# Two output projections finished by token halves: norm sums, broadcasts and the first scaled tiles moved in among the products

## The reference

```python
# first block
h = h + concat([y_attn, y_ret]) @ w_out          # output projection, 1024 x 1024
m = rms_norm(h, ffn_norm_w)
h = h + (silu(m @ w_gate) * (m @ w_up)) @ w_down
# second block
...
h = h + memory_cross_attention(c, m, w_q_cross, w_kv_cross, w_o_cross)  # its last product: 512 x 1024
f = rmsnorm(h, g_ffn)
h = h + (silu(f @ w_gate) * (f @ w_up)) @ w_down
return rmsnorm(h, g_final)

def rms_norm(x, w):
    return x * rsqrt(mean(x * x, -1) + EPS) * w
```

## Time and profile before

| | |
|---|---|
| median of three runs | 2857.78 us |
| the profiled execution | 2857.05 us |
| its span in the trace | 2854.9 us |
| PE busy in the span | 2759.4 us, 97% |
| VectorE busy | 1580.7 us, 55% |
| GpSimd busy | 1333.7 us, 47% |
| ScalarE busy | 911.2 us, 32% |
| mean granted TensorE clock | 0.987 of full speed |

### The profile page before, as it was taken

One profiled execution on the slowest core, in us unless ns is written; L12 is line 12 of the kernel. 1 busy time (PEld: TensorE's weight loads), 2 busy tenths in 40 slices (PEclk: granted clock), 3 DMA queues, 4 the chain that ended last, 5 costly groups with the idle time before them and its releaser, 6 DMA issues. The chain is left out here.

```text
span 2854.9 us, 36940 instructions
## 1 busy us (share of the span) xinstructions
PE 2759.4 (97%) x13908; PEld 2231.2 (78%) x13908; DVE 1580.7 (55%) x2437; ACT 911.2 (32%) x1777; POOL 1333.7 (47%) x1012
## 2 busy tenths in 40 slices
PE   7999999999999999999999899999899999999997
PEld 6777788778888888787766688878787788888886
DVE  6776654865555555613367731243378655555556
ACT  5644431332222322324344410021243322223223
POOL 3322334466656666532222244546614665566653
PEclk9999999999999999999999999999999999999998
DMA  3010111112111111220111011132100111111111
GB/s 132 30 38 31 42 68 39 44 52 63 48 50 54 52 59 52 80 76 30 38 30 32 29 52 52 51 118 67 60 30 30 59 60 45 52 52 55 61 48 67
DMA packets 71376, 151.96 MB, mean 53 GB/s; under 512 B 6448, under 2 KB 29360, under 8 KB 70064
## 3 DMA queue, kind: packets, MB, share of 16 engines
q1 hardware_dynamic: 64256, 123.76, 13.6%
q10 hardware_dynamic: 6960, 26.01, 2.4%
HBM read 141.36 MB, written 8.39 MB: 52 GB/s over the span
## 5 line engine op out<-in xcount | busy, mean ns | idle before, releaser
L650 POOL TENSOR_TENSOR WH<-WRAW,CST 128x512 fp32r<-128x512 f32 x204 | 228.8, 1121 | 874.6 <-PE PS L775 750.1
L773 PE MATMUL PS<-XH,WH 128*128 128x512 f32 x1248 | 513.0, 411 | 2.8 <-DVE XL L2104 2.8
L775 PE MATMUL PS<-XH,WL 128*128 128x512 f32 x1248 | 489.7, 392 | 0.0
L774 PE MATMUL PS<-XL,WH 128*128 128x512 f32 x1248 | 489.0, 392 | 0.0
L684 POOL TENSOR_TENSOR WL<-WRAW,WH 128x512 fp32r<-128x512 f32 x216 | 309.9, 1435 | 272.7 <-ACT WH L1732 271.7
L2543 DVE TENSOR_TENSOR H<-H,PS 128x512 f32<-128x512 f32 x352 | 236.3, 685 | 161.7 <-PE PS L1097 159.3
L773 PEld LDWEIGHTS PS<-XH,WH 128*128 128x128 f32 x1248 | 235.3, 189 | 82.8 <-issue 36.3
L1095 PE MATMUL PS<-HH,WH 128*128 128x512 f32 x704 | 275.5, 391 | 5.3 <-DVE HL L2477 5.3
L1732 ACT ACTIVATE WH<-WRAW 128x512 fp32r<-128x512 f32 x204 | 129.4, 634 | 471.4 <-PE PS L1097 382.9
L652 POOL TENSOR_TENSOR WL<-WRAW,WH 128x512 fp32r<-128x512 f32 x204 | 271.6, 1331 | 16.0
L775 PEld LDWEIGHTS PS<-XH,WL 128*128 128x128 f32 x1248 | 235.4, 189 | 52.0
(11 more groups left out here) (334 smaller groups left out, 4989.4 us busy)
## 6 DMA issues: line engine op xcount, KB each, us to landing
WRAW<-ws SPq DMA_DIRECT2D x104, 512.0 KB, 3.5
WRAW<-ws SPq DMA_DIRECT2D x176, 256.0 KB, 2.6
RAWX<-ws SPq DMA_DIRECT2D x88, 256.0 KB, 2.7
H<-xT ACTq DMA_DIRECT2D x4, 1024.0 KB, 10.9
H<-xT ACTq DMA_DIRECT2D x2, 2048.0 KB, 11.0
h_spill<-H ACTq DMA_DIRECT2D x1, 4096.0 KB, 11.2
H<-h_spill ACTq DMA_DIRECT2D x4, 1024.0 KB, 8.0
outT<-H ACTq DMA_DIRECT2D x4, 1024.0 KB, 4.4
```

Source lines behind the costliest of these rows:

```text
L650: pool.tensor_tensor(WH[:, j, c], WRAW[:, j, c], ONES[:, 0:1].to_broadcast((P, 512)), ALU.mult).then_inc(hi_split, 1)
L773: pe.matmul(out, WH[:, j, w], rh(kt), start=(n == 0), stop=False)
L774: pe.matmul(out, WH[:, j, w], rl(kt), start=False, stop=False)
L775: last = pe.matmul(out, WL[:, j, w], rh(kt), start=False, stop=(n == len(kts) - 1))
```

## The change

Three things, in both transitions:

- The last two units go by halves of the tokens. In the first projection (6,0), (7,0), (6,1), (7,1); in the cross projection the units n = 2 and 3 run all their h = 0 tiles, then all their h = 1 tiles (`CROSS_OUT`, the order for all three engines).
- `norm_sums(k, 0)` and `norm_spread(k, 0)` go in among the products of h = 1 of these units, `norm_sums(k, 1)` from behind the last unit to kt 2 of `plain(0)`, and `norm_spread(k, 1)` from kt 3 to kt 6. Root and inverse of h = 1 go from piece 2 to piece 5.
- The scaled pieces 0 and 1 are taken out of the feed-forward loop (`plain_scale`, `plain_high`): piece 0's scale before the last tile's result is added, piece 1's scale and piece 0's low part between that addition and the last addition of squares. ScalarE makes high part 0 before the last square and high part 1 after it.

In the cross projection ScalarE's table for the square root is also loaded ahead of the tiles, and `add_squares` waits for its own last addition.

```diff
@@ pe
             def norm_sums(k, h):
-                pe.wait_ge(summed, 2 * h + 2 if not k else 16 * k + 4 if h else 16 * k - 4 if k in (2, 5) else 16 * k + 3)
+                pe.wait_ge(summed, 2 * h + 2 if not k else 16 * k + 4 if h else 16 * k + (0, 2, -4, 3, 0, -4)[k])
...
                 for h in range(2):
-                    unit_half(u0 + 6, h)
-                last_unit(u0 + 7, k)
+                    for u in (u0 + 6, u0 + 7):
+                        def hook(kt):
+                            if (u, h, kt) == (u0 + 6, 1, 4):
+                                norm_sums(k, 0)
+                            if (u, h, kt) == (u0 + 7, 1, 2):
+                                norm_spread(k, 0)
+
+                        unit_half(u, h, hook)
...
-                            if b == 0 and h == 0 and kt == 3:
+                            if (b, h, kt) == (0, 0, 2):
+                                norm_sums(k, 1)
+                            if (b, h, kt) == (0, 0, 6):
                                 norm_spread(k, 1)
...
+                def hook(kt):
+                    if (n, second, h, kt) == (2, 0, 1, 0):
+                        norm_sums(4, 0)
+                    if (n, second, h, kt) == (3, 1, 1, 2):
+                        norm_spread(4, 0)
...
-            norm_spread(4, 0)
-            norm_sums(4, 1)
+            for n, second, h in CROSS_OUT:
+                if (n, second, h) != (0, 0, 0):
+                    cross_out(n, second, h)
@@ act
-                for t in (6, 7):
-                    for h in range(2):
+                for h in range(2):
+                    for t in (6, 7):
                         bank = 2 * ((u + t) % 2) + h
                         square(t, h, bank, uses[u + t][bank])
                         if (t, h) == (7, 0):
                             norm_root(k, 0)
+                        if h:
+                            plain_high(t - 6)
...
-                for n in range(16):
-                    kt, h = n % 8, n // 8
-                    if n == 2:
+                for n in range(2, 16):
+                    if n == 5:
                         norm_root(k, 1)
...
+                    plain_high(n)
...
+            load_sqrt()
+            for n, second, h in CROSS_OUT:
@@ dve
+            def plain_scale(k, gain, n):
+                if n < 16:
+                    kt, h = n % 8, n // 8
+                    if n == 5:
+                        norm_inverse(k, 1)
+                    if kt == 0:
+                        dve.wait_ge(spread, 2 * k + h + 1)
+                    dve.scalar_tensor_tensor(out=scaled_input(kt, h), in0=H[:, kt, half(h)], scalar=v(gain + kt),
+                                             in1=PS[:, OB + h], op0=ALU.mult, op1=ALU.mult).then_inc(scaled, 1)
+                    nsc.n += 1
+                if n:
+                    kt, h = (n - 1) % 8, (n - 1) // 8
+                    if n == 16:
+                        dve.wait_ge(scaled, nsc.n)
+                    xh, xl = plain_input(kt, h)
+                    low(xl, scaled_input(kt, h), xh)
...
-                    for t in (6, 7):
-                        for h in range(2):
+                    for h in range(2):
+                        for t in (6, 7):
                             bank = 2 * ((u0 + t) % 2) + h
                             add_result(t, h, bank, uses[u0 + t][bank])
-                            add_squares()
+                            if (t, h) == (7, 1):
+                                plain_scale(k, gain, 1)
+                            add_squares(h)
                             if (t, h) == (7, 0):
                                 norm_inverse(k, 0)
+                            if (t, h) == (6, 1):
+                                plain_scale(k, gain, 0)
...
+                if (n, second, h) == (3, 0, 1):
+                    plain_scale(4, V_GFFN, 1)
+                add_squares(h)
+                if (n, second, h) == (2, 1, 1):
+                    norm_inverse(4, 0)
+                if (n, second, h) == (3, 1, 1):
+                    plain_scale(4, V_GFFN, 0)
```

More of the change, by code:

```diff
@@ L548, in program @@
         U2V, VV, C21, C22 = (XX[:, HALF * n:HALF * (n + 1)] for n in range(4))
+        CROSS_OUT = ([(n, second, h) for n in (0, 1) for second in (1, 0) for h in range(2)]
+                     + [(n, second, h) for h in range(2) for n in (2, 3) for second in (1, 0)])
         def raw(r):
@@ L2055, in _ @@
             split_cross(1)
-            for n in range(4):
+            load_sqrt()
+            for n, second, h in CROSS_OUT:
                 u = U_CO + n
[L2060 to L2065, removed]
+                bank = 4 + h if second else 2 * (u % 2) + h
+                square(2 * n + second, h, bank, uses[u][bank])
+                if (n, second, h) == (3, 0, 0):
+                    norm_root(4, 0)
+                if (n, h) == (3, 1):
+                    plain_high(1 - second)
             ffn(1, 4)
@@ L2087, in link, with add_squares @@
                 dve.wait_ge(dve_step, nst.at())
-            def add_squares():
-                h = nsm.n % 2
+            def add_squares(h=None):
+                sq = nsm.n % 2
+                h = sq if h is None else h
                 dve.wait_ge(squared, nsm.at() + 1)
-                dve.tensor_tensor(ACC[:, h], ACC[:, h], SQ[:, h], ALU.add).then_inc(summed, 1)
+                dve.wait_ge(summed, nsm.at())
+                dve.tensor_tensor(ACC[:, h], ACC[:, h], SQ[:, sq], ALU.add).then_inc(summed, 1)
                 nsm.n += 1
@@ L2417, in residual @@
                     nsm.end(3)
[L2418 to L2419 removed]
+                    for h in range(2):
+                        for t in (6, 7):
                             bank = 2 * ((u0 + t) % 2) + h
                             add_result(t, h, bank, uses[u0 + t][bank])
[L2422 removed]
+                            if (t, h) == (7, 1):
+                                plain_scale(k, gain, 1)
+                            add_squares(h)
                             if (t, h) == (7, 0):
                                 norm_inverse(k, 0)
+                            if (t, h) == (6, 1):
+                                plain_scale(k, gain, 0)
             def ffn(f, k, gain):
                 hid, bases = 44 * f, N_DONE * f
[L2429 to L2436, removed]
[L2437 to L2444 removed]
+                for n in range(2, 17):
+                    plain_scale(k, gain, n)
                 def t_sums(kt):
@@ L2558, in _ @@
             dve.wait_ge(x_in2, 16)
-            residual(U_WO1, 1)
+            residual(U_WO1, 1, V_F1)
             ffn(0, 1, V_F1)
@@ L2766, in _ @@
             clear_sums()
-            for n in range(4):
+            for n, second, h in CROSS_OUT:
                 u = U_CO + n
-                for second in (1, 0):
-                    for h in range(2):
-                        bank = 4 + h if second else 2 * (u % 2) + h
-                        add_result(2 * n + second, h, bank, uses[u][bank])
-                        add_squares()
-                        if (n, second, h) == (3, 0, 0):
-                            norm_inverse(4, 0)
+                bank = 4 + h if second else 2 * (u % 2) + h
+                add_result(2 * n + second, h, bank, uses[u][bank])
+                if (n, second, h) == (3, 0, 1):
[5 more added lines that the diff above has]
+                    plain_scale(4, V_GFFN, 0)
             ffn(1, 4, V_GFFN)
```

27 lines of the change are left out of this document (7 added, 20 removed).

## The result

The median after the change is 2864.66 us (19 runs, 2860.9 to 2866.76) against 2858.62 us before (19 runs beside them, 2857.37 to 2860.04). The forecast was 2861, +3.4; the range of 2852 to 2866 held, but the median lies outside the forecast's own band (2858.5 to 2863.5), in the one given to the mild part of rival B. The 19 runs lie in two heaps, five from 2860.9 to 2861.9 and fourteen from 2863.7 to 2866.8. The profiled execution, 2860.99 us with a span of 2859.1, is of the lower one.

What follows compares the result with a forecast made beforehand. VectorE's chain from the last projection tile to 583 was taken to bound the kernel. First transition +2.0 us, second +1.4, so +3.4 on 2857.05 gave 2860.5, with the runs' median 0.7 higher 2861.2, called 2861; range 2852 to 2866.

Steps and rivals of the forecast that it cites:

- rival B: PE slower: three short idle stretches hold half clock to kt 6, +9 us, 2870; chance 0.18 with the milder part past 2863.5.
- What bounds: VectorE's chain from last projection tile to 583 sets where PE goes on; PE waits some 2 us, 574 to 584.
- When the tile ends: Last projection tile's end after the change (T') against before (T): +0.94 us in the first transition, +0.3 in the second.
- VectorE after T': Behind the last tile, early pieces meet GpSimd: low 0 ends at 3.0 us, low 1 at 6.3, scale 4 at 8.2.
- an uncontested port: If VectorE's early pieces never met GpSimd behind last tile: low 0 at 2.0, low 1 at 4.4, 4 us less together.
- The new waits: VectorE waits at piece 5 for root and inverse, at scale 8 for the spread: scale 8 at 16.35 us, before 13.36.
- the clock: Half clock on PE from about 3 to 10 us behind the last tile, as long as before.
- Rival A: PE's clock stays up in both transitions: spread ends at 14.55, 0.0 us in sum, 2857.8; chance 0.25.
- What comes back: GpSimd's split starts 5.1 us ahead of the gate, so `t_sums(0)` meets fewer operations: 2.9 us won per transition.
- The sum: First transition 0.94 + 1.1 = +2.0, second 0.3 + 1.1 = +1.4, +3.4 us in all.

Runs made afterwards that it cites:

- pe_extra: The kernel before with 9 more PE products (2.04 us) ahead of the first fast product in each feed-forward part; 2858.7 us, ratio 1.0002.
- dve_extra: The kernel before with three more VectorE subtractions ahead of t_sums(1) in each feed-forward part; 2863.68 us, ratio 1.0019.
- pool_late: The changed kernel with GpSimd's split of the third weight quarter held back until low part 0 is made; 2857.17 us, ratio 0.9992.
- filler: The changed kernel with nine PE products whose result is never read, placed where PE stands idle; 2861.06 us, ratio 1.0011.
- again: The changed kernel unchanged, run again for a second profile; 2862.8 us, ratio 1.0019.

## Why the prediction was right, and where it was not

**What bounds.** Right, and shown by *pe_extra* and *dve_extra* for the part of the chain that they touch. PE's waits at the fast products grew from 2.6 to 4.4 us, by 1.8 where I had said 2.0.

**When the tile ends.** In the first transition the last tile started from a point 0.23 us earlier, so T' = T + 0.93 where 0.94 was forecast. The second stands 2.3 us later than before; less the 1.45 us from the first transition and 0.7 us that the profiles differ by in between, 0.2 us are left, where 0.3 was forecast.

**VectorE after T'.** Low 0 ended at T' + 3.0 and low 1 at 6.2, where 3.0 and 6.3 stood; the addition of squares took 1.52 us as it met GpSimd. The bound below, an uncontested port, became real with *pool_late*: low 0 at 2.0, as said there. I had put its worth at 4 us for both transitions together; against *filler* P1 came 2.2 and 2.1 us earlier.

**The new waits.** Both came at the places named: root and inverse ahead of piece 5 (0.25 us, 1.44 in *again*), and the spread ahead of scale 8 (1.93 and 3.42 us, 4.12 in *again*). Scale 8 was forecast at 16.35 and came at 14.8, 16.3 and 18.2. The step that failed here is the clock: I took one stretch from 3 to 10. It was half as long (3.0 to 6.4), or came later (8.6 to 12.0), or lasted longer (3.5 to 13.7), and it changed from one execution to the next. Rival A, no half clock, had the spread end at 14.55; *filler*, which has no half clock, has the spread start at 13.66, and scale 8 there at 14.75 where A had 14.6; A's total of 0.0 was too low all the same, by the term that comes next. Rival B's mechanism, three short idle stretches that hold half clock to kt 6, is what *again* shows in its first transition; I had priced it at 4.5 us, and it cost 3.4 at P1. The sizes of PE's idle were 1.09 for the bank (0.7 by my times) and 1.29 for low 0 (1.8).

**What comes back.** This term was mis-sized, and it is the larger error. I let GpSimd start 5.1 us ahead of the gate and gave VectorE 2.9 us per transition for it. Relative to the gate it started 3.9 us early (539.14 against 543.08): behind the spread PE went as forecast, but the gate did not lose the 1.0 us that I had put ahead of it for the last low parts. GpSimd's operations that VectorE then met took 1.57, 1.62 and 1.49 us, where the first two before took 1.04 and 1.30 (540.48 and 541.60); so GpSimd lost part of its lead. Its last one ended at 554.89, 1.1 us before `t_sums(0)` did (its first three and last operation of after, then its last of before):

```profile
539.14 1.57 POOL L698 TENSOR_TENSOR WH<-RAWX,CST 128x512 fp32r<-128x512 f32 x1 [17.42 <-PE PS L1138]
540.79 1.62 POOL L688 TENSOR_TENSOR WL<-RAWX,WH 128x512 fp32r<-128x512 f32 x1
542.37 1.49 POOL L698 TENSOR_TENSOR WH<-RAWX,CST 128x512 fp32r<-128x512 f32 x1
...
553.34 1.55 POOL L714 TENSOR_TENSOR WRAW<-WRAW 128x512 f32<-128x512 f32 x1
```

```profile
554.14 1.56 POOL L710 TENSOR_TENSOR WRAW<-WRAW 128x512 f32<-128x512 f32 x1
```

In before that last operation outlasted `t_sums(0)`, which ended at 554.55, so fewer than the 8.4 operations of my sum were met there, and fewer could be saved.

`t_sums(0)` went from 12.1 to 11.5 us. From the gate to P1 it is 42.5 us before (42.7 in the second transition) and 41.8 in after, in *again* and in *filler*: 0.7 to 0.9 us came back, not 2.9.

**The sum.** Per transition the forecast was a scale 8 that is 3.0 us later, 1.0 us lost where the last low parts meet GpSimd, and 2.9 us back. Measured with full clock: 1.4 later, nothing lost there, 0.7 to 0.9 back, P1 +0.7 and +0.5. (The last low parts did meet GpSimd, two took 2.57 us together at 540.39; but from scale 15 to the gate it is 3.35 us, as before: there VectorE waited 1.15 us for ScalarE's tanh, and now it doesn't.) With the half clock as it fell in the profile: +0.8 and +2.0. The forecast of +3.4 was near the +4.2 of the profiled span because the delay was put too high and the relief too high as well, which is luck; the +6.0 of the medians is more; the profile of *again* and the runs of *filler* speak for a longer half clock in most executions. The sign was right, and the range held because its upper end took in a part of rival B, whose mechanism *again* shows. Whether the loss is a little under or over 0.2% the interval, 1.0012 to 1.0026, leaves open.

What stays open: why half clock is short in one execution and long in another of the same program, and the 1 to 3 us by which the last tile stands apart from profile to profile.

## What to carry to other kernels

Before filling idle time of the busiest engine, ask which engine it waits for next: here 2 us more of VectorE behind the last tile cost 2 us or more, and 2 us more of PE behind the spread cost next to nothing. A result needed by the pacing engine (here the norm's spread) may move behind other work only as far as the worst clock in between still lets it be in time. When work is moved to start earlier, look at what else starts at the same event: one wait that held GpSimd back until the first early piece was done turned +6.0 us into -1.8 us.

## What the runs showed of the hardware

**Short idle stretches and the clock.** In after, idle stretches of 1.09 and 1.29 us with two products between them were followed by half clock for 3.4 us in one profile and for 10.2 us in another; in the second transition, behind a third stretch of 1.47 us, half clock came at T' + 8.6. With fillers among them (stretches of 0.31 and 1.46 us, in the second transition 0.94 and 1.16) the clock stayed at full, and so it did in *pool_late* (1.09, 0.25 and 0.39 us). The Trainium skill, "TensorE: Matmul & The Clock Gate", section "HAM oscillation — how this bites in real kernels", warns only of idle gaps longer than any of these; the trace does not agree with it as a bound, since here half clock came behind shorter ones that followed one another. Why it lasted 3.4 us once and 10.2 us another time no run shows.

**What a met operation costs.** In these rows VectorE's operations on SBUF alone end 0.55 us behind the GpSimd operation that they meet: GpSimd's first WL of after ended at 518.58 and low 0 at 519.13; in *pool_late* GpSimd's ended at 520.01 and 521.70, low 1 and low 2 at 520.55 and 522.25. The Trainium skill, "SBUF — State Buffer", section "SBUF: two separate sides", says that the loser blocks until the other's instruction is over, and the trace agrees. What I had not expected is how much the order matters: low 0 and the addition of squares, back to back, took 1.73 and 1.52 us, while in *pool_late* low parts that alternate with scales (which read PSUM) took 0.87 and 1.12 us, as part of GpSimd's operation passed under the scale, which took its usual 0.74. Alone each takes 0.69.
